# A two-layer recurrent decoder trunk: the second half of the FFN down products in two parts, norm sums of six outputs, and another order in the out-projection

## The reference

```python
def _layer(x, st, w):
    x = _layer_norm(ALPHA * x + 0.5 * _swiglu(x, w['ffn1_wg'], w['ffn1_wu'], w['ffn1_wd']), w['ln1_g'], w['ln1_b'])
    p = x @ w['w_in']
    ...  # RWKV-7 heads -> ya, mLSTM heads -> yb, and their states
    mix = jnp.concatenate([ya, yb], axis=-1) @ w['w_out']
    x = _layer_norm(ALPHA * x + mix, w['ln2_g'], w['ln2_b'])
    x = _layer_norm(ALPHA * x + 0.5 * _swiglu(x, w['ffn2_wg'], w['ffn2_wu'], w['ffn2_wd']), w['ln3_g'], w['ln3_b'])
    return x, (shift, wkv, conv, C, n, m)
```

## Time and profile before

| | us |
|---|---|
| Time, median of 3 runs (lowest, highest) | 1597.53 (1594.33, 1598.25) |
| Profiled execution, its own time | 1597.23 |
| Its span, first to last instruction | 1595.5 |
| TensorE busy with matmuls | 1525.2 |
| VectorE busy | 975.6 |
| ScalarE busy | 712.1 |
| GpSimd busy | 372.6 |
| Mean granted TensorE clock | 0.970 |

### The profile page before, as it was taken

The page is one execution under the profiler, slowest core; times in us unless marked ns, Lnnn a source line. Parts: engine busy times, 40 slices in busy tenths (PEclk is TensorE's granted clock), DMA queues, the critical chain, the costliest instruction groups (busy, mean ns, idle before and its releaser), DMA issues.

```text
span 1595.5 us, 35416 instructions
## 1 busy us (share of the span) xinstructions
PE 1525.2 (96%) x13914; PEld 1464.9 (92%) x13914; DVE 975.6 (61%) x1568; ACT 712.1 (45%) x1218; POOL 372.6 (23%) x390
## 2 busy tenths in 40 slices
PE   7999998999899899999999999899989998999995
PEld 7999997999778899999999999889978788999994
DVE  4444435578276587775387775466944575777643
ACT  4333335656535443334343334367654355333432
POOL 6222470011241322222122232000132322222110
PEclk9999999999998999999999999999999799999998
DMA  7555542443114555444455445444330444545340
GB/s 207 147 147 151 164 146 70 129 118 95 31 49 118 142 148 154 145 135 145 149 146 156 141 137 173 117 106 107 94 82 3 117 124 118 160 144 153 118 137 33
DMA packets 307948, 197.80 MB, mean 124 GB/s; under 512 B 7616, under 2 KB 283104, under 8 KB 307840
## 3 DMA queue, kind: packets, MB, share of 16 engines
q1 hardware_dynamic: 304224, 189.64, 40.9%
q0 software_dynamic: 3616, 6.62, 1.9%
HBM read 187.46 MB, written 8.78 MB: 123 GB/s over the span
## 4 chain that ended last, share of the span: by engine, by line
PE 85%; DVE 6%; ACT 5%; issue 2%; DVEq 1%; POOL 1%; DMA 0%; ACTq 0%
PE bank L1996 22%; PE bank L1998 22%; PE bank L1997 22%; PE bank L2075 2%; DVE wlo L2444 1%; ACT whi L2258 1%; PE bank L2039 1%; PE bank L586 1%; PE bank L705 1%; PE bank L2080 1%; PE bank L717 1%; POOL xl L2671 1%; PE bank L447 1%; PE bank L610 1%; PE bank L458 1%
## 5 line engine op out<-in xcount | busy, mean ns | idle before, releaser
L2444 DVE TENSOR_TENSOR wlo<-raw,whi 128x1024 fp32r<-128x1024 f32 x340 | 421.9, 1245 | 254.7 <-ACT whi L2258 253.6
L2258 ACT ACTIVATE whi<-raw 128x1024 fp32r<-128x1024 f32 x340 | 357.8, 1057 | 473.1 <-PE bank L1998 463.1
L1996 PE MATMUL bank<-rhi,whi 128*128 128x322 f32 x984 | 306.5, 311 | 0.0
L1998 PE MATMUL bank<-rhi,wlo 128*128 128x322 f32 x984 | 305.9, 311 | 0.0
L1997 PE MATMUL bank<-rlo,whi 128*128 128x322 f32 x984 | 304.8, 310 | 0.0
L1996 PE MATMUL bank<-xh,whi 128*128 128x320 f32 x912 | 286.1, 314 | 5.4 <-DVE wlo L2444 4.0
L1997 PE MATMUL bank<-xl,whi 128*128 128x320 f32 x912 | 283.4, 311 | 0.0
L1998 PE MATMUL bank<-xh,wlo 128*128 128x320 f32 x912 | 283.2, 311 | 0.0
L2681 POOL TENSOR_TENSOR hl<-scratch,hh 128x320 f32 x88 | 146.6, 1665 | 518.7 <-DVE scratch L2560 410.7
L1996 PE MATMUL bank<-hh,whi 128*128 (+1 forms) x704 | 218.6, 310 | 0.5 <-DVE wlo L2444 0.5
L1997 PE MATMUL bank<-hl,whi 128*128 (+1 forms) x704 | 217.4, 309 | 0.0
(11 more groups left out here) (402 smaller groups left out, 2031.2 us busy)
## 6 DMA issues: line engine op xcount, KB each, us to landing
raw<-in_ffn_wg SPq DMA_DIRECT2D x88, 512.0 KB, 3.8
raw<-in_ffn_wu SPq DMA_DIRECT2D x88, 512.0 KB, 3.8
raw<-in_ffn_wd SPq DMA_DIRECT2D x88, 512.0 KB, 3.7
raw<-in_w_in SPq DMA_DIRECT2D x60, 512.0 KB, 3.8
raw<-in_w_out SPq DMA_DIRECT2D x16, 512.0 KB, 6.2
raw<-in_state_C SPq DMA_DIRECT2D x8, 512.0 KB, 6.1
out_s_C<-raw SPq DMA_DIRECT2D x8, 512.0 KB, 3.2
ring<-in_state_wkv POOLq DMA_DIRECT2D x2, 1024.0 KB, 8.3
```

The costliest lines, as they stand in the source:

```text
L1996: pe.matmul(out, w_hi, hi, start=start, stop=False)
L1998: return pe.matmul(out, w_lo, hi, start=False, stop=stop)
L2258: act.activation(whi[:, slot, :], raw[:, slot, :], ACT.Copy).then_inc(hi_ready.sem, 1)
L2444: dve.tensor_tensor(wlo[:, slot, :], raw[:, slot, :], whi[:, slot, :].bitcast(F32), ALU.subtract).then_inc(lo_ready.sem, 1)
```

## The change

The second half of each FFN's down tiles is cut along other lines. Five tiles hold four hidden blocks and two outputs (4 and 5), one tile holds the last two blocks of all four outputs, and five tiles hold four blocks of outputs 6 and 7. So outputs 4 and 5 end in the sixth tile, and their z, squares and raw copies are put near the ninth tile's split. The groups of the norm sums grow from 4 to 6 outputs; the group is summed ahead of the last tile, and not of the last two. The loops over the second half become straight code. In the out-projection the two hand-written orders are replaced: in the turn for output p each engine now splits tile WO + 4 + p, ScalarE ahead of the square and the raw copy, VectorE between z(p) and the raw copy; gain and bias are copied before the turns.

```diff
-        GROUP = (4, KT - 1, 4)
+        GROUP = (6, KT - 1, 6)
+        NPAIR = NDN // 2
+        LAST_DOWN = [(4 * m, 4, 4, 2) for m in range(NPAIR)] + [(4 * NPAIR, 2, 4, 4)] + [
+            (4 * m, 4, 6, 2) for m in range(NPAIR)]
...
+                    for n, (k, rows, o, columns_) in enumerate(LAST_DOWN):
+                        src = wd[bass.ds(L, 1), k * P:(k + rows) * P, o * P:(o + columns_) * P]
+                        load(first + NDN + n, 0, src.rearrange("l (k p) n -> p (l k) n", p=P))
...
+                    def down_part(n, k, o, at, start, stop):
+                        return three_passes(pe, bank[o - 4][:, 0:T], slot_of(L, first + NDN + n), at, hh[:, k, :],
+                                            hl[:, k, :], start, stop)
...
+                    for n, (k0, rows, o0, _) in enumerate(LAST_DOWN):
+                        pe.wait_ge(lo_ready.sem, lo_ready.by(L, first + NDN + n + 1))
+                        if n == NDN - 1:
                             pe.wait_ge(consts.sem, 1)
                             if (L, which) != (0, 2):
                                 ln_sums_of_group(which)
-                        down(first + 2 * RS + 1, 0)
-                        down(first + 2 * RS + 2, 0)
+                        if rows == 4:
+                            for k in range(4):
+                                for o in range(2):
+                                    last = down_part(n, k0 + k, o0 + o, (2 * k + o) * P, n == 0 and k == 0,
+                                                     n == NDN - 1 and k == 3)
+                        else:
+                            for o1 in (0, 2):
+                                for k in range(2):
+                                    for o in (o1, o1 + 1):
+                                        last = down_part(n, k0 + k, o0 + o, (4 * k + o) * P, o1 == 2 and k == 0,
+                                                         o1 == 0 and k == 1)
+                        last.then_inc(used.sem, 1)
...
@@ ScalarE, FFN @@
-                    each(act, base + NUP + NDN + LOOK, NDN - LOOK, split_hi)
+                    for n in range(LOOK, NDN):
+                        split_hi(base + NUP + NDN + n)
+                        if n == NDN - 2:
+                            squares(4, 6, which)
+                            if raw_next:
+                                raw_hi(4, 6, which)
                     for p in follow:
                         split_hi(p)
-                    squares(4, KT, which)
+                    squares(6, KT, which)
...
@@ ScalarE, out-projection @@
                 split_hi(WO + LOOK)
-                split_hi(WO + LOOK + 1)
                 gain_and_bias_hi(1)
-                squares(0, LOOK, 1)
-                raw_hi(0, LOOK, 1)
-                split_hi(WO + LOOK + 2)
-                for p in range(LOOK, KT):
-                    split_hi(WO + p + LOOK)
+                for p in range(KT):
+                    split_hi(WO + LOOK + 1 + p)
                     squares(p, p + 1, 1)
                     raw_hi(p, p + 1, 1)
-                split_hi(U2 + LOOK)
...
@@ VectorE, FFN @@
-                    each(dve, base + NUP + NDN + LOOK, NDN - LOOK, split_lo)
+                    for n in range(LOOK, NDN):
+                        if n == NDN - 2:
+                            residual(4, 6, which, c, 0, lambda o: base + NUP + NDN + NPAIR + 1)
+                        split_lo(base + NUP + NDN + n)
+                        if n == NDN - 2 and raw_next:
+                            raw_lo(4, 6, which)
                     for p in follow:
                         split_lo(p)
-                    residual(4, KT, which, c, 0, lambda o: base + FFN)
+                    residual(6, KT, which, c, 2, lambda o: base + FFN)
...
@@ VectorE, out-projection @@
                 split_lo(WO + LOOK)
-                for p in range(LOOK):
+                gain_and_bias_lo(1, RAW[L, 1])
+                for p in range(KT):
                     mixed(p)
-                split_lo(WO + LOOK + 1)
-                split_lo(WO + LOOK + 2)
-                gain_and_bias_lo(1, RAW[L, 1])
-                raw_lo(0, LOOK - 1, 1)
-                for p in range(LOOK, KT):
-                    split_lo(WO + p + LOOK)
-                    mixed(p)
-                    raw_lo(p - 1, p, 1)
-                raw_lo(KT - 1, KT, 1)
-                split_lo(U2 + LOOK)
+                    split_lo(WO + LOOK + 1 + p)
+                    raw_lo(p, p + 1, 1)
```

More of the change, by code:

```diff
@@ L1949, in ffn, with down @@
                     each(sp, base + RS, NUP - RS, up)
[L1950 to L1957, removed]
+                    first = base + NUP
+                    def down(p, i):
+                        src = wd[bass.ds(L, 1), bass.ds((i * RS + (p - first)) * 2 * P, 2 * P), 0:4 * P]
+                        load(p, i, src.rearrange("l (k p) n -> p (l k) n", p=P))
+                    each(sp, first, NDN, down)
+                    for n, (k, rows, o, columns_) in enumerate(LAST_DOWN):
+                        src = wd[bass.ds(L, 1), k * P:(k + rows) * P, o * P:(o + columns_) * P]
+                        load(first + NDN + n, 0, src.rearrange("l (k p) n -> p (l k) n", p=P))
                 ffn(U1, I["ffn1_wg"], I["ffn1_wu"], I["ffn1_wd"])
@@ L2158, in ffn @@
                                      ident[0:NV2, 0:NV2]).then_inc(vec_turned.sem, 1)
[L2159 to L2182, removed]
@@ new lines, in ffn, with down @@
+                    first = base + NUP
+                    def down(p, i):
+                        pe.wait_ge(lo_ready.sem, lo_ready.by(L, RS * i + p + 1))
+                        pe.wait_ge(hl_done.sem, hl_done.by(L, f * NFF + 2 * RS * i + 2 * (p - first) + 2))
+                        for k2 in range(2):
+                            k = 2 * RS * i + 2 * (p - first) + k2
+                            for o in range(4):
+                                hid = lambda t: (t[:, k, :] if isinstance(i, int) else
+                                                 t[:, bass.ds(k, 1), :].rearrange("p k t -> p (k t)"))
+                                last = three_passes(
+                                    pe, bank[4 + o][:, 0:T], slot_of(L, p), (4 * k2 + o) * P, hid(hh), hid(hl),
+                                    p == first and k2 == 0, p == first + NDN - 1 and k2 == 1)
+                        last.then_inc(used.sem, 1)
@@ new lines, in down_part @@
+                    def down_part(n, k, o, at, start, stop):
+                        return three_passes(pe, bank[o - 4][:, 0:T], slot_of(L, first + NDN + n), at, hh[:, k, :],
+                                            hl[:, k, :], start, stop)
+                    down(first, 0)
+                    each(pe, first + 1, 2 * RS, down)
+                    down(first + 2 * RS + 1, 0)
+                    down(first + 2 * RS + 2, 0)
+                    pe.wait_ge(up_done.sem, up_done.by(L, (f + 1) * NFF))
@@ L2183, in ffn @@
+                    if f == 0:
+                        pe.wait_ge(vec_ready.sem, vec_ready.by(L, 1))
+                    for n, (k0, rows, o0, _) in enumerate(LAST_DOWN):
+                        pe.wait_ge(lo_ready.sem, lo_ready.by(L, first + NDN + n + 1))
+                        if n == NDN - 1:
                             pe.wait_ge(consts.sem, 1)
```

4 lines of the change are left out of this document (2 added, 2 removed).

## The result

The changed kernel takes 1579.41 us, the median of 4 executions (1571.74 to 1584.04), beside 1597.64 for the kernel before (4 executions, 1594.33 to 1598.25). The ratio is 0.9885, 95% interval 0.985 to 0.992: 18.2 us less, where 23.8 were forecast, and 0.4 us above the end of the range. The execution that was profiled is the fastest of the four: 1571.74 us, a span of 1570.0.

What follows compares the result with a forecast made beforehand. TensorE was taken to be held up by the order of two in-order queues at the out-projection's end. 2 x (5.65 + 1.95) = 15.2 plus 4 x 2.15 = 8.6 gave 23.8 us: median 1573.7 us, range 1569.5 to 1579.

Steps and rivals of the forecast that it cites:

- The ring of the out-projection: Out-projection: ScalarE and VectorE splits and z wait on each other, 3.67 us a turn; the new order removes this.
- the clock stays up over its end: Out-projection's end: without the wait TensorE keeps full clock, so FFN2's raw chunks take 1.95 us less per layer.
- four norms are shorter by 2.15 us: FFN norms: TensorE sums two outputs instead of four, 2.15 us less in each of four, 8.6 us together.
- B: FFN norms: late group sum or ScalarE's table load gives back the 8.6 us, time 1582.3; chance 0.05.
- D: FFN second halves: two-column loads set the tiles' pace and the kernel gets slower, up to 1608 us; chance 0.03.
- TensorE's want at 246.0: Layer 0's FFN1: TensorE wants GpSimd's group sum at 246.1; GpSimd's adds were forecast done at 240.4 to 244.7.
- the last one: Whole kernel: 23.8 us off the profiled execution gives span 1571.7, time 1573.4, median 1573.7, own spread 1571.7 to 1575.7.
- C: Behind FFN1's norms: the low-clock stretch moves with the gap, time 1569.9 or 1577.5; chance 0.10.
- The twin: Out-projection: the scaled copy whose 0.55 us was taken as the cost of VectorE's low copy.
- the wait: Out-projection's end: TensorE's wait for the low split of U2+2 goes whole, 5.65 us a layer.
- rival A: Out-projection: VectorE's turns exceed 3.52 us, TensorE still waits some 2 us a layer, time 1578.9; chance 0.09.
- The term for the clock: Raw chunks of FFN2: 14.74 us fall to 12.79 at full clock, 1.95 us a layer.

Runs made afterwards that it cites:

- e1: The changed kernel run again without an edit: median 1575.78 us over 6 executions, ratio 0.9889 to the kernel before.
- e3: The changed kernel with its out-projection hunks undone, so the FFN part alone: median 1588.54 us, ratio 0.9967 to the kernel before.
- e4: The changed kernel with VectorE's low copies of out-projection outputs 3 to 6 moved behind the low split of U2+2: 1573.21 us, ratio 0.9866.
- e6: The changed kernel with FFN norm sums in groups of four outputs as before: 1584.11 us, ratio 0.9916 to the kernel before.
- e8: e3 run once more, beside the kernel before in as many executions: 1592.37 us, ratio 0.9966.
- e9: The kernel before with only the two-column tiles and straight code of the second halves: 1597.54 us, ratio 1.0007.
- e7: The changed kernel with GpSimd summing only outputs 0 to 2 of the out-projection and TensorE the rest: 1580.12 us, one execution.
- e5: e4 plus 30 unused matmuls per layer in TensorE's gap behind the first FFN's norm: 1567.39 us, ratio 0.9807 to the kernel before.
- e11: The kernel before plus 30 unused matmuls per layer in the gap behind the first FFN's norm: 1592.97 us, ratio 0.9991.

## Where the prediction held and where it failed

- The mechanisms that it named were right. The ring of the out-projection is gone, the clock stays up over its end, four norms are shorter by 2.15 us, and no new wait behind the tiles, GpSimd's sums or the transfers came up. B and D did not occur: the sums stop at 241.13 ahead of TensorE's want at 246.0, and 512 KB land in the same 3.7 us.
```profile
raw<-in_ffn_wd SPq DMA_DIRECT2D x88, 512.0 KB, 3.7
```
- The failed step is the last one: "Span 1571.7, time 1573.4, median **1573.7 us**", with "Its own spread, from runs that lie 4 us apart". It takes all that the change doesn't touch as constant. In-projection and mixers are not: 503.7 to 516.0 in the four executions of the changed kernel, and in the mean 2.7 to 4.4 us longer than in before in each of the six kernels that have the tiles, an idle gap and more than one execution (e1, e3, e4, e6, e8, e9). Of the first comparison, the mean is 18.3 us less than before's: 22.6 less in the fixed stages, some 4.3 more in the recurrent ones. Three executions that lay 4 us apart had hidden how far they move; the 18 beside e1 lie 12 us apart (1590.63 to 1602.74). Why they are longer in the mean is open, as said above. C had the right idea, that a moved gap moves the clock, but looked only at the 4.2 us behind the gap, where nothing changed, and not at the 250 us of each layer behind, in which a stretch has the lower clock in one profile and not in another (at 461, above).
- Mis-sized: "VectorE has z 0.49, the split 1.34 and the low copy, taken at 0.55 as its twin, 2.4 us, or 2.7 with the longest split". It was 2.90: the low copy takes 1.16, as each one begins while an add of GpSimd is under way, and so does each split. The twin was ScalarE's scaled copy, 0.55 at 542.43, which takes that long although an add of GpSimd (542.10 to 543.20) runs beside it; it tells nothing of VectorE. In the ring of the kernel before, VectorE's own low copies took 0.54, but each began ahead of the add, and there the add was the longer one (1.12 for 0.88):
```profile
530.86 0.54 DVE L2475 SCALAR_TENSOR_TENSOR rlo<-z,vec,rhi 128x320 fp32r<-128x320 f32 x1
...
531.02 1.12 POOL L2694 TENSOR_TENSOR scratch<-scratch,z 128x320 f32<-128x320 f32 x1 [2.58 <-DVE z L2452]
```
- So VectorE's turns stayed below the 3.52 us, but it never caught up with its late start; the last split came 0.78 us late, and the wait lost 4.72 us a layer and not 5.65: 1.9 us of the sum. This is rival A's mechanism at a third of its size, and without its loss of clock. The term for the clock, 1.95, measured 1.90. This error alone would have left the median inside the range.
- The terms of the sum then measure 2 x (4.72 + 1.90) + 8.6 = 21.8 for 23.8, and the fixed stages 22.6. Of the 0.8 between, 0.6 is at the very end: the final 24 transposes take 4.28 us for 4.88 (the rows are before's, then the changed kernel's). The granted clock is 0.51 in the first 4.33 us of them in before, in the first 3.08 in the changed kernel, and 1.00 in the rest; half of that difference is 0.6. No term of the sum had it.
```profile
1586.57 4.88 PE L2241 MATMUL bank<-ident,x 128*128 128x128 f32 x24 [13.98 <-ACT x L2298]
...
1561.62 4.28 PE L2260 MATMUL bank<-ident,x 128*128 128x128 f32 x24 [13.99 <-ACT x L2317]
```
- Luck had a part in both directions. The profiled execution, forecast as 1573.4, took 1571.74, because its recurrent stages happened to be 2.9 us shorter than those of before's profile. And six more executions of the same kernel (e1) have a median of 1575.78, inside the range: with executions that lie 16 us apart, on which side of 1579 a median of four falls is in part chance. That the mean gain is 18 us and not 23.8 came both times.
- The sum and the range thus needed a term for all stretches with a clock under 1.00: the earlier trace rows and the page showed some, and the mixers' rows, which I hadn't read, show 0.93 and 0.88.

## What to carry to other kernels

Split the span into stages whose time is arithmetic and stages in which the clock falls, judge the terms of a change in the first by stage times of one profile, and give the second a spread of its own. A change that only shifts work can cost or win some us there, so a part that is worth less than that shows in stage times long before it shows in a median. Cost an instruction by one of the same engine, and look at which engine's instruction was under way when it began.

## What was not expected of the hardware

- VectorE beside GpSimd, same shapes: the split of 128x1024 takes 1.22 us or 1.50, the low copy of 128x320 0.54 or 1.16 to 1.18, GpSimd's add of 128x320 0.87 or 1.67 to 1.94. It isn't enough that the other engine is at work: the one that begins second is the longer. In the changed kernel a split that begins 0.17 us ahead of an add takes 1.22 and the add 1.79 (rows below). In e7 a low copy that begins 0.82 us before an add's end (531.18 + 1.51) takes 0.63 more than the 0.54 alone. z, which reads a bank, takes 0.48 with or without an add beside it. The Trainium skill (GPSIMD Engine Reference, Key points) has the shared interface, and these traces agree.
```profile
522.74 1.22 DVE L2463 TENSOR_TENSOR wlo<-raw,whi 128x1024 fp32r<-128x1024 f32 x1
...
522.91 1.79 POOL L2711 TENSOR_TENSOR scratch<-z 128x320 f32<-128x320 f32 x1 [7.72 <-DVE z L2471]
```
- 30 matmuls into a bank that nobody reads, in a gap of 4.9 us, kept 2.4 GHz for what follows in the profiles of e5 and e11 (15 matmuls that were 0.267 apart in before are 0.147 apart in e5, but for two).
- The same 0.9 us of idleness in the same place of the mixers is followed by 10 us at 1.2 GHz in one profile and by none in another (the rows of before and e9 at 461).
